# Sample attention: the selection bias added by TensorE from one copy on the chip, and other gather orders

## What is computed

```python
# per sample b and new position t, over L = 4096 cached + 8 new keys
s = einsum('bqhd,bsd->bqhs', q_idx, k_idx)
s = einsum('bqhs,bqh->bqs', relu(s), w_idx)        # index score
sel = top_k(where(k_pos <= q_pos, s, -inf), 256)
s = einsum(q, k[sel]) * 64**-0.5 - slope[h] * (q_pos - sel)   # 8 heads, 2 KV heads
o = einsum(softmax(s), v[sel])
```

## Time and profile before

| | us |
|---|---|
| median of 3 runs | 3179.17 |
| lowest and highest | 3177.24, 3183.16 |
| profiled execution | 3177.16 |
| its span, first to last instruction | 3175.3 |

### The profile page before, as it was taken

How to read it: one execution, slowest core, us unless ns; L and a number is a source line. 1 busy time by engine, 2 the same in 40 slices (tenths; PEclk the granted TensorE clock), 3 DMA queues, 4 the chain that set the end, 5 groups by cost and what they waited for, 6 DMA issues and landing times. The chain is left out here.

```text
span 3175.3 us, 31772 instructions
## 1 busy us (share of the span) xinstructions
PE 2804.5 (88%) x11426; PEld 1492.8 (47%) x11426; DVE 1994.0 (63%) x3979; ACT 811.0 (26%) x1537; POOL 33.8 (1%) x41
## 2 busy tenths in 40 slices
PE   5659999999999999999999998799995569898896
PEld 4645444444455454454545454455553344343344
DVE  3320588897798898988989887228981224424422
ACT  2210232233333323333333333321002211201201
POOL 0000000000000000000000000100000000000000
PEclk9779999999999999999999999899997789999996
DMA  2130211111111110111010100223127558224115
GB/s 85 61 73 15 52 50 37 37 38 35 43 38 38 41 38 28 33 32 39 26 39 27 37 26 23 66 86 141 58 61 217 156 178 288 88 111 165 53 30 21
DMA packets 196290, 215.18 MB, mean 68 GB/s; under 512 B 80304, under 2 KB 161840, under 8 KB 191984
## 3 DMA queue, kind: packets, MB, share of 16 engines
q1 hardware_dynamic: 192688, 171.34, 18.8%
q0 software_dynamic: 3456, 41.94, 3.9%
HBM read 157.53 MB, written 55.72 MB: 67 GB/s over the span
## 5 line engine op out<-in xcount | busy, mean ns | idle before, releaser
L815 PE MATMUL attn_ps_r<-xT,attn_w_rest 128*128 128x424 f32 (+2 forms) x2240 | 906.8, 547 | 14.0 <-DMA attn_w_rest<-in_w_in 7.7
L115 DVE TENSOR_SCALAR_CACHE_REDUCE attn_hits<-attn_acc,attn_search_bits 128x384 uint8<-128x384 f32 (+13 forms) x434 | 641.6, 1478 | 11.8
L815 PEld LDWEIGHTS attn_ps_r<-xT,attn_w_rest 128*128 128x128 f32 x2240 | 405.6, 191 | 417.1 <-issue 407.8
L1096 PE MATMUL sidx_ps_r<-xT,samp_w_rest 128*128 128x424 f32 (+1 forms) x720 | 260.4, 525 | 11.3 <-DMA samp_w_rest<-in_w_in 11.3
L1678 PE MATMUL merge_ps_y<-merge_w_out,merge_merged 128*128 128x512 f32 (+1 forms) x544 | 236.9, 598 | 0.0
L735 DVE SCALAR_TENSOR_TENSOR attn_acc<-attn_ps_s,iw,attn_acc 128x512 f32<-128x512 f32 (+3 forms) x266 | 181.9, 684 | 65.9 <-ACT attn_ps_s L662 43.4
L870 PE MATMUL attn_ps_p<-ident,attn_prob 128*128 128x128 f32 x1088 | 166.3, 291 | 50.9 <-ACT attn_prob L679 45.5
L1666 PE MATMUL merge_ps_u<-merge_attn,merge_up_a 128*128 128x512 f32 (+1 forms) x320 | 135.7, 596 | 85.4 <-DVE merge_attn L1710 81.2
L1096 PEld LDWEIGHTS sidx_ps_r<-xT,samp_w_rest 128*128 128x128 f32 x720 | 138.9, 193 | 131.8 <-issue 120.2
L679 ACT ACTIVATE attn_prob<-attn_prob,attn_lowest 128x128 f32<-128x128 f32 (+15 forms) x128 | 152.8, 1194 | 183.0 <-DVE attn_lowest L752 182.9
L870 PEld LDWEIGHTS attn_ps_p<-ident,attn_prob 128*128 128x128 f32 x1088 | 126.1, 147 | 155.6 <-ACT attn_prob L679 67.0
(11 more groups left out here) (248 smaller groups left out, 2614.6 us busy)
## 6 DMA issues: line engine op xcount, KB each, us to landing
rest_t<-attn_rest SPq DMA_DIRECT2D x108, 212.0 KB, 2.0
attn_w_rest<-in_w_in SPq DMA_DIRECT2D x35, 512.0 KB, 4.1
merge_gates<-rest_t SPq DMA_DIRECT2D x8, 2048.0 KB, 11.6
norm_x_in<-in_x_prompt SPq DMA_DIRECT2D x16, 512.0 KB, 3.7
attn_w_rest<-in_w_in SPq DMA_DIRECT2D x32, 256.0 KB, 3.9
merge_x<-in_x_prompt SPq DMA_DIRECT2D x4, 2048.0 KB, 7.9
out_y_prompt<-merge_y SPq DMA_DIRECT2D x16, 512.0 KB, 2.6
rest_t<-samp_rest SPq DMA_DIRECT2D x36, 212.0 KB, 2.0
```

The lines of the kernel that those rows point to most:

```text
L115: self.v.done(self.nc.vector.tensor_scalar(self.hits, self.x, limit, None, op, ALU.add, accum_out=self.count))
L815: ins = nc.tensor.matmul(bank(g)[:, 0:width], w_rest[:, j % 2, k, :], c.xT[:, k, t0:t0 + width], start=(k == 0), stop=(k == KC - 1))
L1096: last = nc.tensor.matmul(ps_r[:, i % 2, 0:width], w_rest[:, j % 2, kc, :], c.xT[:, kc, t0:t0 + width], start=(kc == 0), stop=(kc == KC - 1))
```

## The change

The bias is no longer stored, replicated and loaded back. It stays in `score`, 64 rows. VectorE builds, in the search program ahead of the index scores, a matrix `spread` of zeros and ones that has, for every sample, a 1 where a row (sample, position) belongs to a column (head, position). For each chunk TensorE adds to the scores in the same bank of PSUM the product of `spread` and the chunk of the bias, a 64 by 64 multiply for each half. VectorE's `move` is then one operation of one tensor, score times slope with the chunk's own minimum, into a buffer that no longer comes filled; the new keys move behind the last chunk of their pair, and one more small operation takes the minimum over all parts before the exponential (`lowered`). The second buffer of `reps` is new space (`extra`), under `work` and `sets`.

The gathers change as well: pair 1's four go out at the end of the search program, when the last projection step is done on TensorE (its input `xT` is then free), and in attention the keys of pairs 2 and 3 are queued ahead of the values of pairs 2 and 3. AHEAD becomes 5.

```diff
@@ stage_sample
-        k.work = m.sb("work", [P, 2048])
-        k.sets = m.sb("sets", [P, 2048])
+        k.extra = m.sb("extra", [P, KEYS])
+        k.work, k.sets = (k.extra[:, n * 2048:(n + 1) * 2048] for n in range(2))
+        k.spread = m.sb("spread", [ST, DB, NH, DT])
-        k.reps = [k.bias, k.score]
+        k.reps = [k.bias, k.extra]
-def load_bias(eng, a, k, i, half):
...
@@ sample_select
-        AHEAD = 8
-        bias_after = len(steps) - 5
+        AHEAD = 5
...
-                    if i == bias_after:
-                        sp.wait_ge(made, 2)
-                        sp.dma_start(a["bias_s"], score).then_inc(bias_out, 16)
-                        sp.wait_ge(bias_out, 16)
-                        load_bias(sp, a, o, 0, 0)
-                        load_bias(sp, a, o, 0, 1)
...
                 pool.wait_ge(o.k_in[0], 32)
                 pool.wait_ge(o.v_in[0], 32)
                 pool.dma_reset()
+                pool.wait_ge(rest_done, len(steps))
+                for u in range(2):
+                    gather(pool, o, o.stores[1][:, 0, u, :], o.k_src, 2 + u, o.k_in[1])
+                for u in range(2):
+                    gather(pool, o, o.stores[1][:, 1, u, :], o.v_src, 2 + u, o.v_in[1])
...
+                v.done(nc.vector.tensor_scalar(same_b[:], step8[:], low[:, 1:2], None, ALU.is_equal))
+                for b in range(DB):
+                    v.done(nc.vector.tensor_scalar(o.spread[:, b], same_t[0:ST, :].unsqueeze(1).to_broadcast([ST, NH, DT]),
+                                                   same_b[0:ST, b:b + 1], None, ALU.mult))
@@ sample_attend, gpsimd
-                for i in range(1, PAIRS):
-                    if i >= 2:
-                        pool.wait_ge(turned, 2 * NC * (i - 1))
+                for i in range(2, PAIRS):
+                    pool.wait_ge(turned, 2 * NC * (i - 1))
                     for u in range(2):
                         gather(pool, o, stores[i % 2][:, 0, u, :], o.k_src, 2 * i + u, o.k_in[i])
-                    if i >= 2:
-                        pool.wait_ge(weighted, NC * (i - 1))
+                for i in range(2, PAIRS):
+                    pool.wait_ge(weighted, NC * (i - 1))
                     for u in range(2):
                         gather(pool, o, stores[i % 2][:, 1, u, :], o.v_src, 2 * i + u, o.v_in[i])
@@ sync
-                load_bias(sp, a, o, 1, 0)
-                load_bias(sp, a, o, 1, 1)
-                for i in range(2, PAIRS):
-                    sp.wait_ge(p_turned, NC * (i - 2) + NC // 2)
-                    load_bias(sp, a, o, i, 0)
-                    sp.wait_ge(p_turned, NC * (i - 1))
-                    sp.wait_ge(new_turned, i - 1)
-                    load_bias(sp, a, o, i, 1)
@@ tensor, scores(g)
-                    r = g + i + 1
-                    if ch == 0:
...
+                    r = g + i
                     if r >= 2:
                         pe.wait_ge(moved, r - 1)
                     pe.wait_ge(kept, 2 * g + 2)
                     for u in range(2):
-                        last = nc.tensor.matmul(ps_s[u * NR:(u + 1) * NR, r % 2, :], q_bd[:, 2 * i + u, :],
-                                                keysT[:, g % 2, u, :], start=True, stop=True)
+                        nc.tensor.matmul(ps_s[u * NR:(u + 1) * NR, r % 2, :], q_bd[:, 2 * i + u, :],
+                                         keysT[:, g % 2, u, :], start=True, stop=False)
+                    for u in range(2):
+                        last = nc.tensor.matmul(ps_s[u * NR:(u + 1) * NR, r % 2, :], spread[:, 2 * i + u, :],
+                                                bias[:, ch * 512:(ch + 1) * 512], start=False, stop=True)
                     last.then_inc(multiplied, 1)
+                    if ch == NC - 1:
+                        pe.wait_ge(moved, r)
+                        for u in range(2):
+                            nc.tensor.matmul(ps_s[u * NR:(u + 1) * NR, (r + 1) % 2, 0:ST], q_bd[:, 2 * i + u, :],
+                                             c.ksT[:], start=True, stop=False)
...
@@ scalar, exponential
-                        act.wait_ge(moved, (NC + 1) * (i + 1))
+                        act.wait_ge(lowered, i + 1)
@@ vector, move(g)
...
-                    nc.vector.tensor_tensor_reduce(
-                        out=cols, in0=ps_s[:, r % 2, :], in1=cols, scale=slope[:], scalar=low[:, ch:ch + 1],
-                        op0=ALU.add, op1=ALU.min, accum_out=low[:, ch + 1:ch + 2]).then_inc(moved, 1)
+                    nc.vector.tensor_scalar(rep[:, ch * 512:(ch + 1) * 512], ps_s[:, r % 2, :], slope[:], None,
+                                            ALU.mult, ALU.min, accum_out=low[:, ch:ch + 1]).then_inc(moved, 1)
+                    if ch == NC - 1:
+                        dve.wait_ge(multiplied, r + 2)
+                        nc.vector.tensor_scalar(rep[:, PAST:KEYS], ps_s[:, (r + 1) % 2, 0:ST], slope[:], None,
+                                                ALU.mult, ALU.min, accum_out=low[:, NC:NC + 1]).then_inc(moved, 1)
+                        dve.wait_ge(moved, r + 2)
+                        nc.vector.tensor_reduce(low[:, NC + 1:NC + 2], low[:, 0:NC + 1], AX_X, ALU.min
+                                                ).then_inc(lowered, 1)
```

More of the change, by code:

```diff
@@ L948, in stage_sample @@
         k.v_in = [m.sem(f"v_in{i}") for i in range(PAIRS)]
-        k.b_in = [[m.sem(f"b_in{u}{half}") for half in range(2)] for u in range(2)]
         k.k_src = a["cache_k"].rearrange("l n (q t) h d -> (l n q) (t h d)", q=QT)
         k.v_src = a["cache_v"].rearrange("l n (q t) h d -> (l n q) (t h d)", q=QT)
-        k.reps = [k.bias, k.score]
+        k.reps = [k.bias, k.extra]
+        k.stores = [k.cache, c.xT[:].rearrange("p k t -> p (k t)")[:, 0:4 * TPR * P].rearrange(
+            "p (i u n) -> p i u n", i=2, u=2)]
         sample_select(nc, c, a, k)
@@ L1000, in sample_select @@
         (tabled, stored, spread_in, zeroed, masked, numbered, rowed, gathered, selected, turned, kept, scored, rectified,
-         summed, read, positioned, made, bias_out, own, rest_done, rest_kept) = [m.sem(n) for n in (
+         summed, read, positioned, own, rest_done, rest_kept) = [m.sem(n) for n in (
             "tabled", "stored", "spread_in", "zeroed", "masked", "numbered", "rowed", "gathered", "selected", "turned",
-            "kept", "scored", "rectified", "summed", "read", "positioned", "made", "bias_out", "own", "rest_done",
+            "kept", "scored", "rectified", "summed", "read", "positioned", "own", "rest_done",
             "rest_kept")]
@@ L1248, in _ @@
                 dve.wait_ge(positioned, 1)
[L1249 removed]
+                v.done(nc.vector.scalar_tensor_tensor(
                     score[:, 0:PAST].rearrange("r (v p) -> r p v", v=TPR), kpos.rearrange("r (p v) -> r p v", v=TPR),
[L1251 to L1252 removed]
+                    low[0:ST, 0:1], chosen[:, 0:PAST].rearrange("r (p v) -> r p v", v=TPR), ALU.add, ALU.add))
                 v.done(nc.vector.tensor_tensor(score[:, PAST:KEYS], chosen[:, PAST:KEYS], newpos[:], ALU.subtract))
[L1254 to L1255 removed]
+                v.done(nc.vector.scalar_tensor_tensor(score[:, PAST:KEYS], later[:], BIG / MASKED, score[:, PAST:KEYS],
+                                                      ALU.mult, ALU.add))
 def sample_attend(nc, c, a, o):
@@ L1261, in sample_attend @@
         m = Stage(nc, ctx, "satt")
-        spare = c.xT[:].rearrange("p k t -> p (k t)")[:, 0:4 * TPR * P].rearrange("p (i u n) -> p i u n", i=2, u=2)
-        stores = [o.cache, spare]
+        stores = o.stores
         def by_key(i, which):
@@ L1271, in sample_attend @@
         q_bd, slope, attT = o.q_bd, o.slope, o.attT
+        bias, spread = o.score[0:ST], o.spread[:].rearrange("r b h t -> r b (h t)")
         probT_new = m.sb("probT_new", [ST, P])
-        lowest = m.sb("lowest", [P, 2, NC + 1])
+        lowest = m.sb("lowest", [P, 2, NC + 2])
         rowsum = m.sb("rowsum", [P, 2, 2])
@@ L1350, in scores @@
                     for u in range(2):
-                        last = nc.tensor.matmul(ps_s[u * NR:(u + 1) * NR, r % 2, :], q_bd[:, 2 * i + u, :],
-                                                keysT[:, g % 2, u, :], start=True, stop=True)
-                    last.then_inc(multiplied, 1)
+                        nc.tensor.matmul(ps_s[u * NR:(u + 1) * NR, r % 2, :], q_bd[:, 2 * i + u, :],
[3 more added lines that the diff above has]
+                                                bias[:, ch * 512:(ch + 1) * 512], start=False, stop=True)
+                    last.then_inc(multiplied, 1)
+                    if ch == NC - 1:
[3 more added lines that the diff above has]
+                                             c.ksT[:], start=True, stop=False)
+                        for u in range(2):
+                            last = nc.tensor.matmul(ps_s[u * NR:(u + 1) * NR, (r + 1) % 2, 0:ST], spread[:, 2 * i + u, :],
```

(2 more changed lines are left out.)

28 lines of the change are left out of this document (10 added, 18 removed).

## The result

The changed kernel took 3160.88 us (median of 5 runs, 3159.39 to 3164.14) against 3178.53 (5 runs, 3174.73 to 3183.16) before: ratio 0.9945, 95% interval 0.9931 to 0.9960. It is faster by 17.7 us, half of the 35.7 forecast, and lies above the range of 3130 to 3158.

The account below looks back on a forecast made before the run. TensorE sets the pace except in two holes, the barrier before attention and waits in attention. Gains 10.9 + 31.2 + 18.5 + 10.8 less costs 33.0, 0.9, 0.8 and 1.0 give 35.7 us: 3143.5 us forecast, range 3131 to 3153 (with store rival 3130 to 3158).

Parts of the forecast that it names:

- forecast of 2391.5: Start of attention on TensorE at 2391.5 us, a gain of 10.9 us, with bounds 14.5 and -3.
- Last store: End of the search program: the last projection store, sharing the DMA engines with four gathers, lands 6.6 us after it starts.
- rule of turns: Each DMA engine alternates packet by packet between queue rows with work, so the store gets through among the first gather packets.
- The rival in which the store waits behind the gathers: End of search program: store lands at about 2402, attention starts at 2404, gain 12.5 us less, 3156 us; chance 0.11.
- Five steps ahead: Projections: AHEAD 8 to 5 makes the index part start late, waiting for index-key gathers and ScalarE; cost 1.7 us.
- Gather waits: Attention: TensorE's two waits for key gathers, pairs 1 and 3, both go through earlier issue and new order; 31.2 us gained.
- Bias waits: Attention: two waits of the scores for VectorE, which stood for the replicated bias, go; 18.5 us gained.
- restarts: Attention: after each of four waits TensorE runs at its lower clock level, losing 2.7 us each; 10.8 us gained.
- Bias multiplies: Attention: two 64-row multiplies per chunk, running side by side, cost 1.03 us for each of 32 chunks, 33.0 us in all.
- Small terms: Attention costs: first scores at low clock 0.9 us, new keys' multiplies 0.8, key copies behind the exponential ending pair 0 1.0.
- a gather still late: Attention: one of two K waits with its restart stays, for example pair 1's; 18 us less gain, 3161.5 us; chance 0.05.
- a hole above 18 us: Sign against the prediction: TensorE's hole before attention, 22 us before and forecast at about 9, stays above 18 us.

## Why the prediction was wrong

The step that failed is one clause: "Each of GpSimd's gathers holds it 1.24 us (0.94 and 0.30), some 5 us in all, so it comes to the barrier at 2385 at the earliest." It came there at 2407.1. The row of 0.94 us is the time of an issue, and I used it as the time for which a gather can hold GpSimd's program. No row of before showed a GpSimd program that ends with gathers under way, because each waited for them by name first; the change made the first one. That was a wait that the trace of before does not show, and it should have been bounded as such: from the issue of the last gather (about 2384) to its landing, by the V gathers of 18.7 us in the earlier trace rows about 2403 or later. I gave the last store that bound and GpSimd none. The runs settle it: without the drain the start is at 2386.6, with two gathers at 2399.8, with four at 2409.4. Against the forecast of 2391.5 that is 17.9 us late, a loss of 7.0 against the start before (2402.44), outside the bounds of +14.5 and -3 that the prediction gave. 35.7 less 17.9 is 17.8, and the medians gave 17.7; that they agree to 0.1 is luck. In the profiled executions the gain was 16.3 (3177.16 to 3160.88), since the work behind attention took 1.2 us longer there. Nor is the drain's own price 17.9: it is 21.2 (a hole of 26.30 against 5.10), of which the last store, mis-sized the other way, hid 4.6.

The Trainium skill (Perfetto Trace Analysis, section DMA Instruction — SWDGE (GPSIMD)) says that the record of such an instruction ends when its last descriptor is written, not when the data has moved. The trace agrees: 0.94 us of record against 8.8 to 19.8 us to the landing. That the engine's drain waits for the latter is what the runs here add.

The other steps, in the order of the sum:

- *Last store, 6.6 us (2.0 to 20):* it took 2.0, the lower end. It goes out 0.3 us behind the first gather's issue, and by the DMA records all of its 144 packets start from 2384.4 to 2385.4, before the first packet of a gather (2385.4). So the two did not meet, and the rule of turns that the prediction cites from the Trainium skill (DMA: Bandwidth & Descriptors, section Queues, rings and completion order) is not tested by it; no run here shows it. The rival in which the store waits behind the gathers had the right place and the wrong mechanism.
- *Five steps ahead, 1.7 us (0 to 3):* 2.6, by the projections' 336.1 and 338.7 us, and up to 3.8 with the other runs with five steps (up to 339.9); the two waits are those that it named. That VectorE's earlier end is worth nothing held: it is done at 2354.2 now, 29 us ahead of TensorE.
- *Gather waits, 31.2 us:* gone, as forecast, but all save 2.2 for another reason than the places and the order of the gathers: the bias loads no longer share the DMA engines, and a step is longer. The order is worth 3.8 us of attention.
- *Bias waits, 18.5, and restarts, 10.8:* gone; the granted clock of attention is 0.98, and of TensorE's waits there, once it has started, the longest is 1.3 us.
- *Bias multiplies, 33.0 us (29 to 62):* 33.7 net by leaving them out. The steady step came to 4.50 us instead of 4.3 to 4.4, because scores and weighing beside the new group lost 0.10 and 0.05 us too.
- *Small terms:* attention came to 155.6 us from first transpose to last output copy, 24.5 less than the 180.1 before, where the terms of that stretch sum to 24.8. The prediction's 154 does not follow from its own figures: its 179.8 less 24.8 is 155.0. The one at the end of pair 0 (1.0) shows as a wait of 0.3.

The rival "a gather still late" gave 3161.5, 0.6 us from the median, and is still wrong: no wait for a gather stands in the list above. The sign that came is another that the prediction named, a hole above 18 us.

## What to carry to other kernels

A gather moved ahead of the end of its engine's program was awaited there: ask of each asynchronous start that crosses a barrier what closes the program behind it, and price that wait from issue to landing, not by the record of the issue. Either start it behind the barrier, or let that barrier go by semaphores; here each gave 36 to 37 us over the kernel before with five steps ahead, and 40 with eight (3137 us; the one behind the barrier with the old order of the gathers), where the change as made gave 18. And when one transfer is taken away, price the waits for the others without it before you spend an edit on their order: adding the bias on TensorE and taking its replicated loads away was by itself worth 40 us, and of the edits to the gathers the new order saved 3.8 us of attention, which the whole kernel did not show, and the earlier start cost 21.

## What was not expected of the hardware

- GpSimd's drain at the end of a program took 23.94 us behind four gathers of 2 MB and 14.38 behind two, each time until 0.1 to 0.2 us past the last landing, and 0.04 with none under way; work that stood behind a gather in GpSimd's program, the MEMSET at 2055.38 before, did not wait for it.
- Without the drain, GpSimd's sequencer runs ahead of its own gathers: it was clearing semaphores while the fourth was still to be issued.
- Gathers that have the DMA engines to themselves land 4.9 us apart (8.8, 12.5, 16.1 and 19.8 us from issues 1.24 us apart). In the kernel before, beside the bias loads, the first key gather of pair 1 landed 20.5 us after its issue at 2403.06 and the second 31.6 us after its own.
